# A two-block fp32 model on one core: another order of plain chunks and seven-product groups in the down projections

## The reference, cut to what matters

```python
v = rms_norm(h, norm_ffn[l])
h = h + (jax.nn.silu(v @ w_ffn_gate[l]) * (v @ w_ffn_up[l])) @ w_ffn_down[l]
```

## Time and profile before

| | us |
|---|---|
| median of three runs | 2877.25 |
| lowest, highest | 2876.98, 2878.07 |
| the profiled execution's own time | 2878.37 |
| its span | 2876.6 |
| PE busy in the span | 2861.7 |
| DVE busy | 2178.1 |
| ACT busy | 1396.4 |
| mean granted TensorE clock | 0.998 of full |

### The profile page before, as it was taken

One profiled execution on the slowest core, in us unless ns is written; L12 is line 12 of the kernel. 1 busy time (PEld: TensorE's weight loads), 2 busy tenths in 40 slices (PEclk: granted clock), 3 DMA queues, 4 the chain that ended last, 5 costly groups with the idle time before them and its releaser, 6 DMA issues.

```text
span 2876.6 us, 31986 instructions
## 1 busy us (share of the span) xinstructions
PE 2861.7 (99%) x12750; PEld 2361.1 (82%) x12750; DVE 2178.1 (76%) x3008; ACT 1396.4 (49%) x1784; POOL 66.3 (2%) x115
## 2 busy tenths in 40 slices
PE   9999999999999999999999999999999999999999
PEld 7888888888888878888888888888888887888877
DVE  6887777788867788667787866677887768857677
ACT  5554445444544444544446665444454444544443
POOL 1000000000000000010001000000000000000000
PEclk9999999999999999999999999999999999999999
DMA  7555555555555556675555555555555555555555
GB/s 283 188 191 200 186 193 183 200 197 194 194 196 195 190 187 218 220 245 190 192 193 194 176 175 197 177 181 186 188 205 191 189 200 176 210 195 187 199 180 176
DMA packets 84405, 562.22 MB, mean 195 GB/s; under 512 B 10093, under 2 KB 10113, under 8 KB 19744
## 3 DMA queue, kind: packets, MB, share of 16 engines
q1 hardware_dynamic: 77328, 542.71, 54.6%
q0 software_dynamic: 4192, 12.70, 1.4%
q10 hardware_dynamic: 2736, 4.78, 0.5%
HBM read 558.03 MB, written 3.69 MB: 195 GB/s over the span
## 4 chain that ended last, share of the span: by engine, by line
PE 95%; DVE 3%; ACT 1%; issue 1%; DMA 1%; SPq 0%; DVEq 0%; ACTq 0%
PE acc L698 92%; PE misc L698 3%; DVE spare L1714 1%; DVE w_lo L1575 1%; DMA raw<-in_w_in 1%; DVE sum_raw L1575 1%; ACT w_hi L1124 0%; ACT sum_hi L1101 0%; PE misc L703 0%; DVE heads_turned L1714 0%; DVE sum_lo L1575 0%; DVE silu L1581 0%; ACT junk L1087 0%; ACT stage L1082 0%; DVE decay L1578 0%
## 5 line engine op out<-in xcount | busy, mean ns | idle before, releaser
L1575 DVE TENSOR_TENSOR w_lo<-raw,w_hi 128x1024 fp32r<-128x1024 f32 (+2 forms) x989 | 1197.6, 1217 | 531.4 <-ACT w_hi L1124 525.8
L1124 ACT ACTIVATE w_hi<-raw 128x1024 fp32r<-128x1024 f32 x987 | 1035.0, 1055 | 1077.7 <-PE acc L698 1063.3
L698 PE MATMUL acc<-w_hi,u_hi 128*128 128x512 f32 (+1 forms) x1472 | 581.3, 395 | 2.3 <-DVE w_lo L1575 1.4
L698 PE MATMUL acc<-w_hi,u_lo 128*128 128x512 f32 (+1 forms) x1472 | 571.0, 388 | 0.0
L698 PE MATMUL acc<-w_lo,u_hi 128*128 128x512 f32 (+1 forms) x1472 | 570.4, 387 | 0.0
L698 PE MATMUL acc<-w_hi,v_hi 128*128 128x512 f32 x1408 | 548.5, 390 | 0.2
L698 PE MATMUL acc<-w_hi,v_lo 128*128 128x512 f32 x1408 | 548.0, 389 | 0.0
L698 PE MATMUL acc<-w_lo,v_hi 128*128 128x512 f32 x1408 | 548.0, 389 | 0.0
L698 PEld LDWEIGHTS acc<-w_hi,u_hi 128*128 128x128 f32 x1472 | 276.8, 188 | 62.0 <-DVE w_lo L1575 3.6
L698 PEld LDWEIGHTS acc<-w_hi,u_lo 128*128 128x128 f32 x1472 | 276.7, 188 | 57.4
L698 PEld LDWEIGHTS acc<-w_lo,u_hi 128*128 128x128 f32 x1472 | 277.1, 188 | 55.2
(11 more groups left out here) (349 smaller groups left out, 2896.9 us busy)
## 6 DMA issues: line engine op xcount, KB each, us to landing
raw<-in_w_gates SPq DMA_DIRECT2D x112, 1024.0 KB, 4.9
raw<-in_w_ffn_gate SPq DMA_DIRECT2D x88, 1024.0 KB, 4.8
raw<-in_w_ffn_up SPq DMA_DIRECT2D x88, 1024.0 KB, 4.8
raw<-in_w_in SPq DMA_DIRECT2D x66, 1024.0 KB, 4.8
raw<-in_w_ffn_down SPq DMA_DIRECT2D x64, 1024.0 KB, 4.8
raw<-in_w_out SPq DMA_DIRECT2D x32, 1024.0 KB, 4.8
raw<-in_w_branch SPq DMA_DIRECT2D x24, 1024.0 KB, 4.7
raw<-in_w_sums_f SPq DMA_DIRECT2D x22, 1024.0 KB, 4.8
```

The costliest lines, as they stand in the source:

```text
L698: return e.matmul(o, w, x, start=start, stop=stop, skip_group_check=True)
L1124: e.activation(m.w_hi[:, n % PART_SLOTS, 0:HALF_KT * cols], m.raw[:, c % RAW_SLOTS, o * cols:(o + HALF_KT) * cols], ACT.Copy).then_inc(s[" ...
L1575: return e.tensor_tensor(o, a, b, op)
```

## The change

The order of the pieces of a pair is written down in `ORDERS`, and it changes for the first pair of each of the three parts: E E S E S E O S O S O O with four sums, E E S E O S E O S O O with three. The second pairs keep their order. A block's pieces are now a `script`, and the script of the even block takes in all pieces up to the last E or S, whichever comes later (`cut`), chunks of the odd block among them. So the odd block's script in a first pair holds the last two O chunks alone: four halves with four sums, three halves with three. `opens` says which matmul overwrites an accumulator, whatever comes first. No engine gets another instruction or loses one; chunks are loaded in the new order.

```diff
@@ -26,6 +26,7 @@
+ORDERS = {4: ("EESESEOSOSOO", "ESESESESOOOO"), 3: ("EESEOSEOSOO", "ESESESEOOOO")}
@@ -64,7 +67,8 @@
-                                    sums=sums if pairs and j % 2 == 0 else None))
+                                    sums=sums if pairs and j % 2 == 0 else None,
+                                    order=ORDERS[pairs][j // 2] if pairs else ""))
@@ -87,42 +91,62 @@
         for i, b in enumerate(self.blocks):
...
-            for n_chunk, k in enumerate(range(b.k0, b.k0 + b.kn, CHUNK_KT)):
-                n = min(CHUNK_KT, b.k0 + b.kn - k)
-                for o in range(0, n, HALF_KT):
-                    self.half_at.append(len(self.pieces))
-                    self.pieces.append(("half", len(self.halves)))
-                    self.halves.append((len(self.chunks), o, b.cols))
-                self.chunks.append((b.name, b.b, k, n, b.cols))
-                self.split_done.append(("w_lo_done", len(self.halves)))
-                if b.sums and n_chunk < b.sums[2]:
...
+        for i, b in enumerate(self.blocks):
+            if b.sums:
+                self.add_pair(b, self.blocks[i + 1])
+            elif not b.lead:
+                for n in range(-(-b.kn // CHUNK_KT)):
+                    self.add_chunk(b, b, n)
+            b.sums_done = len(self.sum_chunk)
+
+    def add_chunk(self, to, b, n):
+
+        k = CHUNK_KT * n
+        tiles = min(CHUNK_KT, b.kn - k)
+        for o in range(0, tiles, HALF_KT):
+            to.script.append((len(self.pieces), b, (k + o) // HALF_KT, None))
+            self.pieces.append(("half", len(self.halves)))
+            self.halves.append((len(self.chunks), o, b.cols))
+        b.done = len(self.halves)
+        self.chunks.append((b.name, b.b, b.k0 + k, tiles, b.cols))
+        self.split_done.append(("w_lo_done", len(self.halves)))
...
+    def add_pair(self, even, odd):
+
+        even.first_sum = len(self.sum_chunk)
+        taken = {"E": 0, "O": 0, "S": 0}
+        cut = 1 + max(even.order.rindex("E"), even.order.rindex("S"))
+        for i, kind in enumerate(even.order):
+            to = even if i < cut else odd
+            if kind == "S":
+                self.add_sum(to, even)
+            else:
+                self.add_chunk(to, even if kind == "E" else odd, taken[kind])
+            taken[kind] += 1
...
@@ -748,24 +778,29 @@
         products(m6[:, :], s2, *t2, first)
-        products(c21, a22, *t4, False).then_inc(s["sum_read"], 1)
+        open_acc(b)
+        products(c21, a22, *t4, opens(b, 1)).then_inc(s["sum_read"], 1)
         lanes.step()
         e.wait_ge(s["sum_lo_done"], 3 * n + 3)
         products(m1[:, :], a11, *b11, first)
-        products(c11, a12, *b21, False)
-        if first and odd.before:
-            need((f"acc_freed{odd.slot}", odd.before))
-        products(c12, s4, *b22, first).then_inc(s["sum_read"], 1)
+        products(c11, a12, *b21, opens(b, 0))
+        open_acc(odd)
+        products(c12, s4, *b22, opens(odd, 0)).then_inc(s["sum_read"], 1)
...
-    def stream(b):
...
+    def stream(script):
+        for at, b, j, n in script:
+            if n is not None:
+                sum_products(b, n)
+                continue
+            open_acc(b)
...
@@ -1622,18 +1649,13 @@
-    def stream(b):
-        for j in range(b.n):
-            split_ahead(plan.half_at[b.first + j])
+    def stream(script):
+        for at, b, j, n in script:
+            split_ahead(at)
             for i in range(HALF_KT):
-                lanes.until(b.left, b.lead + HALF_KT * j + i)
+                lanes.until(b.left, 2 * (n - b.first_sum) + i if j is None else b.lead + HALF_KT * j + i)
             lanes.step()
-            n = plan.sum_after(b, j)
-            if n is not None:
-                split_ahead(plan.sum_at[n])
-                for i in range(2):
-                    lanes.until(b.left, 2 * (n - b.first_sum) + i)
-                lanes.step()
+            if j is None:
                 lanes.step()
```

More of the change, by code:

```diff
@@ L37, with __init__ @@
 class Block:
-    def __init__(self, label, name, b, k0, kn, cols, left, frees=1, lead=0, sums=None):
+    def __init__(self, label, name, b, k0, kn, cols, left, frees=1, lead=0, sums=None,
+                 order=""):
         self.label, self.name, self.b, self.k0, self.kn, self.cols = label, name, b, k0, kn, cols
         self.left, self.frees, self.lead, self.sums = left, frees, lead, sums
+        self.order = order
 def stream_plan():
@@ L89, in __init__ @@
         self.chunks, self.halves, self.split_done = [], [], []
-        self.pieces, self.half_at, self.sum_at, self.sum_chunk = [], [], [], []
+        self.pieces, self.sum_chunk = [], []
         handed, self.pairs = [0, 0], 0
         for i, b in enumerate(self.blocks):
-            b.first, b.n = len(self.halves), b.kn // HALF_KT
-            b.done = b.first + b.n
-            b.slot = i % 2
+            b.n, b.slot, b.script = b.kn // HALF_KT, i % 2, []
             b.before = handed[b.slot]
@@ L98, in __init__ @@
             b.after = handed[b.slot]
-            b.pair, b.first_sum = self.pairs, len(self.sum_at)
-            for n_chunk, k in enumerate(range(b.k0, b.k0 + b.kn, CHUNK_KT)):
-                n = min(CHUNK_KT, b.k0 + b.kn - k)
-                for o in range(0, n, HALF_KT):
-                    self.half_at.append(len(self.pieces))
-                    self.pieces.append(("half", len(self.halves)))
-                    self.halves.append((len(self.chunks), o, b.cols))
-                self.chunks.append((b.name, b.b, k, n, b.cols))
-                self.split_done.append(("w_lo_done", len(self.halves)))
-                if b.sums and n_chunk < b.sums[2]:
[L109 to L113, removed]
@@ L114, in __init__ @@
-            b.sums_done = len(self.sum_chunk)
+            b.pair = self.pairs
             if b.lead and not b.sums:
                 self.pairs += 1
+        for i, b in enumerate(self.blocks):
[15 more added lines that the diff above has]
+        self.split_done.append(("w_lo_done", len(self.halves)))
@@ new lines, in add_sum @@
+    def add_sum(self, to, b):
+        n = len(self.sum_chunk)
+        to.script.append((len(self.pieces), b, None, n))
+        self.pieces.append(("sum", n))
+        self.sum_chunk.append(len(self.chunks))
+        self.chunks.append((b.sums[0], b.sums[1] + n - b.first_sum, 0, CHUNK_KT, BW))
+        self.split_done.append(("sum_lo_done", 3 * (n + 1)))
+    def add_pair(self, even, odd):
[9 more added lines that the diff above has]
+            taken[kind] += 1
+        n = -(-even.kn // CHUNK_KT)
+        assert taken == {"E": n, "O": n, "S": even.sums[2]} and even.order[-1] == "O", (even.label, taken)
@@ L118, in __getitem__ @@
     def __getitem__(self, label):
         return self.blocks[self.at[label]]
[L121 to L125, removed]
 class Lanes:
@@ L256, in mixing @@
                 gate, branch = plan[f"gate{mark}{n}{c}"], plan[f"branch{mark}{n}{c}"]
-                stream(gate)
+                stream(gate.script)
                 if mark:
@@ L263, in mixing @@
                 lanes.finish(tasks[n])
-                stream(branch)
+                stream(branch.script)
                 if mark:
@@ L273, in residual @@
             b = plan[name]
-            stream(b)
+            stream(b.script)
             if b.lead and not b.sums:
@@ L292, in ffn @@
                 evacuate("ffn_gate", gate, mark, block + j)
-                stream(up)
+                stream(up.script)
                 evacuate("ffn_up", up, gate, mark, block + j)
@@ L310, in walk @@
         if b == 5:
-            stream(plan["keep_misc"])
+            stream(plan["keep_misc"].script)
             evacuate("keep_misc", plan["keep_misc"])
             task("diff")
-        stream(plan[f"keep{b}"])
+        stream(plan[f"keep{b}"].script)
         if b == 0:
@@ L675, in tensor_program @@
     lanes = Lanes()
-    ready, seen = {}, {}
+    ready, seen, opened = {}, {}, set()
     bank_free = [None] * 4
@@ L719, in last_half, with opens @@
         lanes.step()
+    def opens(b, t):
+        if (b.label, t) in opened:
+            return False
+        opened.add((b.label, t))
+        return True
     def products(o, left, right_hi, right_lo, first):
@@ L754, in sum_products, with open_acc @@
         products(m1[:, :], a11, *b11, first)
-        products(c11, a12, *b21, False)
-        if first and odd.before:
-            need((f"acc_freed{odd.slot}", odd.before))
-        products(c12, s4, *b22, first).then_inc(s["sum_read"], 1)
+        products(c11, a12, *b21, opens(b, 0))
+        open_acc(odd)
+        products(c12, s4, *b22, opens(odd, 0)).then_inc(s["sum_read"], 1)
         bank_free[2] = bank_free[3] = ("sums_added", SUM_OUT("r22", pair))
         lanes.step()
-    def stream(b):
+    def open_acc(b):
         if b.before:
             need((f"acc_freed{b.slot}", b.before))
-        v = m.acc[b.slot]
-        left_hi, left_lo = m.left[b.left]
-        for j in range(b.n):
```

(26 more changed lines are left out.)

1 line of the change is left out of this document (removed).

## The result

The changed kernel takes 2890.54 us, the median of six runs (2887.82 to 2891.36), against 2877.51 us before (2876.98 to 2878.53, six runs). The ratio is 1.0044, with a 95% interval of 1.0031 to 1.0057: slower by 13.0 us. The profiled execution took 2891.3 us, with a span of 2889.5.

The account below looks back on a forecast made before the run. PE was taken as the bound, 99% busy, with gaps caused by DVE. Gaps and clock falls: twice 7.45 (four sums) plus 10.15 (three) make 25.1 us instead of 12.9, so 2889.4 us; range 2881 to 2892.

Parts of the forecast that it names:

- What bounds the kernel, and what the gaps cost: PE, 99% busy, loses 4.3 us at each of three old `w_lo` gaps, slower clock included: 12.9 us.
- DVE's new list at the head: First pair on DVE: `silu` at 1031.5, ahead of the first sum split at 1035.7; second sum split at 1050.4.
- Gap at the second sum chunk, four sums: First pair: PE waits 2.1 us for the late second split, then 0.4 and 0.35; together 2.85 us.
- Gap in the third E, three sums: First pair: the third E's second half waits for `hidden_lo`, behind an O half's low part: 3.25 us.
- Into the second pair: PE's first products wait for `r22`, queued behind a sum split on DVE: 2.15 us (four sums), 3.7 (three).
- The clock: PE's clock falls from 2.4 to 1.2 GHz after each of the six new gaps, costing 1.6 us each.
- Loads, flags, scripts at nothing: Reordered loads stay hidden, `opens` only moves a flag, matmuls, splits and transfers keep their number: no cost.
- The rival with closed gaps: No gap left if DVE begins the second split by 1048.4 and `r22` ends in time: 2864.4 us, chance 0.08.

Follow-up runs that it names:

- e4: Changed kernel with three E chunks ahead of the second sum chunk, first one early, and all `sums_out` additions ahead of the second pair's first sum split: 2865.22 us.
- e5: Changed program with the old orders written into `ORDERS`: 2877.77 us, ratio to before 1.0001.
- e7: Changed kernel with the second sum chunk one O chunk earlier in the three-sum part, ahead of `hidden_lo` on VectorE: 2896.11 us.
- e1: Changed kernel with all eight VectorE additions of `sums_out` issued in its second step, ahead of the split of the second pair's first sum chunk: 2878.72 us.
- e3: Changed kernel with the old head of the first pairs (second sum chunk again after one E) and the change's short tail: 2885.84 us.

## Why the prediction was right

It gave 2889.4 us in a range of 2881.0 to 2892.0; 2890.54 was measured. By its steps:

- *What bounds the kernel, and what the gaps cost.* 12.9 us in three gaps. e4, without them, is 12.65 us below its kernel before. Right, though not every one of the three is followed by a fall (e5); where none is, a later short wait takes part of its place.
- *DVE's new list at the head.* Foretold: silu 1031.5, first sum split 35.7, second 1050.4. Measured: 1031.34, 1035.59 and 1050.49, in a trace that runs 0.17 us ahead there (a half's low part at 1026.91 instead of 1027.08). Right, and the idle time ahead of `silu` is there too.
- *Gap at the second sum chunk, four sums.* Foretold 2.1, 0.4 and 0.35. Measured from start to start less one step: 1051.91 to 1054.43 is 2.3 us. The profile shows 2.13 and 2.21 us idle. In this first gap, which no fall follows, the two later terms can be read too: they are smaller than foretold, about 0.3 and 0.1 us (1057.06 to 1057.56, 1059.50 to 1059.83). From 1051.91 to 1059.83, 22 steps, PE lost 2.9 us in all, as the sum of the three had it (2.85). The gap is shown; that DVE starts the second split late because the first one no longer fills its wait ahead of `silu` is read from its list, and no run takes it apart from the rest.
- *Gap in the third E, three sums.* Foretold 3.25, measured 3.50 idle: the term is under-sized, by 0.3 to 0.4 us, mostly because a low part ahead of transposes took 1.25 us from start to start (1047.41 to 1048.66 in f1), not the 1.14 I had used. The mechanism is shown by e7.
- *Into the second pair.* Foretold 2.15 and 3.7; measured 1.85 and 1.84 idle, and 3.37; from start to start it is some 0.17 more. Off by 0.1 to 0.2. The mechanism is shown by e1 (waits gone) and e3 (waits there with the old head).
- *The clock.* Foretold: a fall after each of six. In the profile five gaps are followed by one, and one of these has two slow stretches (2.8 us), so the falls cost about 9.2 us where 9.6 was foretold. That the sum came out is partly luck. As a statement about one gap it was wrong: in e3 only one of six was followed by a fall. All six runs of the changed kernel have a mean granted clock of 0.996 or 0.997, so many falls in each; why it has more of them than e3 with the same tail is not known. The term should have been a range of 0 to 1.6 us each, with the point inside it. The reason given for the fall, that 2.1 us is nearer to 2.68 than to 0.55, does not hold up either: between 1.8 and 3.5 us the share of gaps with a fall does not grow with the gap (last section). The rule of the Trainium skill (TensorE: Matmul & The Clock Gate, Why this matters for your kernels), which warns of idle gaps above about 3 us, is no bound either: here gaps of 1.85 us were followed by a fall, and one of 3.37 us (e3) and one of 3.49 us (e1) were not.
- *Loads, flags, scripts at nothing.* Right (e5). One load was late where I had named another: in the three-sum part DVE waited 1.32 us for a sum chunk's raw data at 2804, without any wait of PE.

The rival with closed gaps fell at its first condition: the second sum split could not begin by 1048.4. It needed another order (e4), with the first sum chunk left where DVE is idle, one more chunk ahead of the second, and the additions moved.

## What to carry to other kernels

When a planner's look-ahead is counted in pieces, a longer piece moved by one place delays everything that stands behind it in an in-order engine's list: here a 7 us split was put ahead of 1.4 us of additions that PE waited for. Before an order is changed, write the helper engine's list out with its times from the trace, at the start and at the seam to the next group, and compare it with when the matmuls want each item. Fill idle time of the helper (the first sum chunk ahead of `silu`) and give it cover (more chunks ahead of the second): e4 did both, and no run tells how much each is worth.

## What was not expected of the hardware

A fall of TensorE's clock to 1.2 GHz behind a short idle gap is not certain, and in this range it does not follow the gap's length. In the profiled executions of all ten versions, 7 of 10 gaps in the down projections of 1.84 to 1.86 us were followed by a fall, 7 of 10 of 2.13 to 2.21 us, 7 of 10 of 2.48 to 2.56 us and 4 of 6 of 3.37 to 3.50 us; the one of 9.27 us was, those of 0.33 us were not. What decides it is open. Most versions with gaps differ more from run to run (10 us over e3's six runs, 3.5 us over the changed kernel's) than the one without (0.7 us); with the old orders it is 1.1 us. Nine or sixteen idle matmuls in a wait kept the clock up all three times in the profiled execution. About three gaps in ten keep it up without them, so these three alone are no proof; the median, 6.2 us lower over eight runs, speaks for it too.
